# A hybrid decoder trunk on one core: four small moves in layer 0, and operand tiles placed at whole kilobytes

## The reference

```python
# layer 0: a recurrent branch beside a latent attention, one output projection
z = rms_norm(h) @ w_in                       # 1024 x 1440
xr, gate, q_lat, kv_lat, k_rope = split(z)
y_lru = rg_lru(xr, gate)                     # conv of 4 taps, two sigmoid gates, a scan over tokens
q  = rms_norm(q_lat) @ w_qb                  # 8 heads of 64 + 32 (rotary)
kv = rms_norm(kv_lat) @ w_kvb                # 64 for keys, 64 for values per head
y_mla = causal_softmax_attention(q, k, v)
h = h + concat(y_lru, y_mla) @ w_out
# layer 1: mLSTM in chunks instead; after either layer
u = causal_conv3(rms_norm(h) @ w_up)         # 1024 -> 2 x 2816
h = h + (silu(u_gate) * u_value) @ w_down
```

## Time and profile before

| | us |
|---|---|
| median of 3 runs | 2345.33 (2345.32 to 2349.07) |
| the profiled execution | 2344.9 |
| its span, first to last instruction | 2342.5 |
| TensorE busy | 2280.9 (97%) |
| VectorE busy | 1330.9 (57%) |
| GpSimd busy | 1028.1 (44%) |
| ScalarE busy | 903.5 (39%) |
| DMA | 122 MB, 52 GB/s over the span |

### The profile page before, as it was taken

How to read it: one execution, slowest core, us unless ns; L and a number is a source line. 1 busy time by engine, 2 the same in 40 slices (tenths; PEclk the granted TensorE clock), 3 DMA queues, 4 the chain that set the end, 5 groups by cost and what they waited for, 6 DMA issues and landing times.

```text
span 2342.5 us, 31827 instructions
## 1 busy us (share of the span) xinstructions
PE 2280.9 (97%) x10415; PEld 1853.4 (79%) x10415; DVE 1330.9 (57%) x2181; ACT 903.5 (39%) x1595; POOL 1028.1 (44%) x711
## 2 busy tenths in 40 slices
PE   8998999999999999999999999999999999999997
PEld 6686777778888888888878878878788888888886
DVE  6846565258655555555671115663875555555556
ACT  4535555124433333333441114451443333333333
POOL 2413333423555555555443422224335555555554
PEclk9999999999999999999999999999999999999998
DMA  5100000311111111111231110012101111111112
GB/s 180 42 18 1 1 0 28 117 36 46 39 52 54 54 49 49 48 50 54 69 124 50 45 45 28 28 73 81 30 35 55 54 54 52 46 51 47 54 54 90
DMA packets 34583, 122.07 MB, mean 52 GB/s; under 512 B 3840, under 2 KB 3968, under 8 KB 34240
## 3 DMA queue, kind: packets, MB, share of 16 engines
q1 hardware_dynamic: 31616, 106.44, 14.6%
q10 hardware_dynamic: 2880, 14.49, 1.6%
HBM read 112.52 MB, written 8.39 MB: 52 GB/s over the span
## 4 chain that ended last, share of the span: by engine, by line
PE 87%; DVE 6%; ACT 3%; issue 2%; POOL 1%; DMA 1%; SPq 0%; ACTq 0%; DVEq 0%; POOLq 0%
PE ps L816 10%; PE ps L814 10%; PE ps L818 9%; PE ps L736 9%; PE ps L738 9%; PE ps L737 9%; PE ps L854 6%; PE ps L855 6%; PE ps L856 6%; PE ps L1572 2%; PE ps L1719 1%; PE ps L1723 1%; PE ps L1721 1%; PE ps L1560 1%; DMA stage<-in_wt 1%
## 5 line engine op out<-in xcount | busy, mean ns | idle before, releaser
L516 POOL TENSOR_TENSOR wlo<-stage,whi 128x512 fp32r<-128x512 f32 x308 | 397.5, 1296 | 462.3 <-ACT whi L979 457.7
L736 PE MATMUL ps<-ahi,whi 128*128 128x512 f32 x896 | 368.5, 411 | 17.3 <-DVE alo L2239 10.3
L435 POOL TENSOR_TENSOR whi<-stage,cons 128x1024 fp32r<-128x1024 f32 x64 | 127.4, 1991 | 548.6 <-PE ps L738 338.2
L738 PE MATMUL ps<-ahi,wlo 128*128 128x512 f32 x896 | 350.4, 391 | 0.0
L737 PE MATMUL ps<-alo,whi 128*128 128x512 f32 x896 | 350.0, 391 | 0.0
L979 ACT CAST whi<-stage 128x512 fp32r<-128x512 f32 x308 | 189.1, 620 | 363.6 <-POOL stage L529 180.6
L1239 DVE TENSOR_TENSOR hT<-hT,ps 128x512 f32<-128x512 f32 x352 | 238.7, 685 | 153.9 <-PE ps L856 153.9
L854 PE MATMUL ps<-hid_hi,whi 128*128 128x512 f32 x640 | 252.2, 394 | 0.7 <-POOL wlo L516 0.2
L855 PE MATMUL ps<-hid_lo,whi 128*128 128x512 f32 x640 | 249.8, 390 | 0.0
L856 PE MATMUL ps<-hid_hi,wlo 128*128 128x512 f32 x640 | 249.7, 390 | 0.0
L814 PE MATMUL ps<-ahi,whi 128*128 128x512 f32 x608 | 236.7, 389 | 0.0
(11 more groups left out here) (324 smaller groups left out, 4096.9 us busy)
## 6 DMA issues: line engine op xcount, KB each, us to landing
stage<-in_wt SPq DMA_DIRECT2D x184, 512.0 KB, 3.6
hT<-in_xt SPq DMA_DIRECT2D x16, 256.0 KB, 6.9
hT<-in_xt ACTq DMA_DIRECT2D x8, 512.0 KB, 7.5
spill<-hT ACTq DMA_DIRECT2D x1, 4096.0 KB, 12.1
hT<-spill ACTq DMA_DIRECT2D x8, 512.0 KB, 8.6
out<-hT SPq DMA_DIRECT2D x16, 256.0 KB, 2.1
wqb_s<-in_wqb ACTq DMA_DIRECT2D x1, 1024.0 KB, 5.2
wlru_s<-in_wlru SPq DMA_DIRECT2D x1, 512.0 KB, 10.8
```

The costliest lines, as they stand in the source:

```text
L516: nc.gpsimd.tensor_tensor(block_lo(c), src, block_hi(c).bitcast(F32), ALU.subtract).then_inc(sem(L + "b_ready"), 1)
L736: nc.tensor.matmul(bank, hi, rhs_k[0][:, tok], start=k_first, stop=False)
L738: return nc.tensor.matmul(bank, lo, rhs_k[0][:, tok], start=False, stop=k_last)
```

## The change

It has five parts. First, the arena: `base` is rounded to 128 bytes, `nw` is rounded up to a whole kilobyte (109 KB), and `xc`, `rt2`, `qf`, `upg`, `upv`, `cvg` and `h1` get new offsets; all pieces, `hid_hi` and `hid_lo`, `lat` and the attention's tiles then start at whole kilobytes, `upv` does not. Second, `reduced()` goes behind `branch_conv(0)`, `branch_in(1)` and `gate_in(0)`. Third, GpSimd makes the rests of all four recurrent outputs, VectorE none. Fourth, ScalarE's list at the start of the attention has another order: `lat_hi` is made later, one tile at a time, each after GpSimd's rest of the tile whose place it takes. Fifth, the recurrent part of output tile m = 0 (eight `product3`, four feature tiles by two token halves) is issued between the steps 4 to 7 of the last head, into banks 2 and 4; the rest of that tile follows behind the head.

```diff
@@ arena
-        base = -(-nc.sbuf_base // 32) * 32
+        base = -(-nc.sbuf_base // 128) * 128
-        nw = -(-c0 // 32) * 32
+        nw = -(-c0 // KB) * KB
-        xc = at("xc", sh + 36 * KB + 32, [P, S])
+        xc = at("xc", sh + 37 * KB, [P, S])
-        upg = at("upg", f1, [P, S + 2])
-        upv = at("upv", f1 + 4 * KB + 32, [P, S + 2])
-        cvg = at("cvg", f1 + 8 * KB + 64, [P, S])
-        h1 = f1 + 12 * KB + 64
+        cvg = at("cvg", f1, [P, S])
+        h1 = f1 + 4 * KB
+        upg = at("upg", h1 + 34 * KB, [P, S + 2])
+        upv = at("upv", h1 + 38 * KB + 32, [P, S + 2])
@@ GpSimd
-            for n, j in enumerate((0, 1)):
-                lru_rest(j, n + 3)
+            for j in range(LRU_T):
+                lru_rest(j, j + 1)
@@ VectorE
             branch_in(0)
-            reduced()
             branch_conv(0)
             branch_in(1)
             gate_in(0)
+            reduced()
...
-            for n, j in enumerate((2, 3)):
-                dve.wait_ge(sem("act_hi"), n + 1)
-                nc.vector.tensor_tensor(alo[:, j, :], ylru[:, j, :], ahi[:, j, :].bitcast(F32),
-                                        ALU.subtract).then_inc(sem("dve_lat"), 1)
@@ VectorE, dve_out
-                    nc.vector.tensor_tensor(h, h, ps[:, 2 * (1 - m % 2) + s, :], ALU.add).then_inc(sem(L + "res"), 1)
+                    bank = 2 + 2 * s if m == 0 else 2 * (1 - m % 2) + s
+                    nc.vector.tensor_tensor(h, h, ps[:, bank, :], ALU.add).then_inc(sem(L + "res"), 1)
@@ ScalarE
-            for j in (2, 3, 0, 1):
+            for j in range(LRU_T):
                 nc.scalar.copy(ahi[:, j, :], ylru[:, j, :]).then_inc(sem("act_hi"), 1)
...
-            act.wait_ge(sem("dve_lat"), 4)
-            for k in range(2):
+            values_out(3)
+            act.wait_ge(sem("dve_lat"), 2)
+
+            def latent_hi(k):
+                act.wait_ge(sem("lru_split"), k + 3)
                 nc.scalar.copy(lat_hi[:, k, :], lat[:, k, :]).then_inc(sem("act_hi"), 1)
-            values_out(3)
+
+            first_query_hi(0, 1)
             nope(0, 0, first_banks[0], 3)
             values_out(4)
-            first_query_hi(0, 1)
+            latent_hi(0)
+            values_out(5)
+            latent_hi(1)
+            values_out(6)
             first_query_hi(1, 0)
-            values_out(5)
-            for c in range(6, TT):
-                values_out(c)
+            values_out(7)
@@ TensorE
+            fillers = {4: ((0, 0),), 5: ((0, 1), (1, 0)), 6: ((0, 2), (1, 1)), 7: ((0, 3), (1, 2), (1, 3))}
+
+            def out_filler(s, k):
+                if (s, k) == (0, 0):
+                    pe.wait_ge(w_ready, T_L0_OUT + 1)
+                    pe.wait_ge(sem("lru_split"), LRU_T)
+                product3(ps[:, 2 + 2 * s, :], slice(k * P, (k + 1) * P), slot_of(T_L0_OUT),
+                         (ahi[:, k, :], alo[:, k, :]), k == 0, False, halves[s])
...
+                    if last and par == 1 and k in fillers:
+                        for filler in fillers[k]:
+                            out_filler(*filler)
                     weigh(p * 2 + par, k, step, grp)
...
-            for m in range(KT):
+            for s in range(2):
+                pe.wait_ge(sem("L0res"), s + 1)
+                for k in range(LRU_T, KT):
+                    last_pair_turned(k, s)
+                    mm = product3(ps[:, 2 + 2 * s, :], slice(k * P, (k + 1) * P), slot_of(T_L0_OUT),
+                                  (ahi[:, k, :], alo[:, k, :]), False, k == KT - 1, halves[s])
+                mm.then_inc(half_done if s == 0 else w_used, 1)
+            for m in range(1, KT):
```

More of the change, by code:

```diff
@@ L183, in build @@
         rt1 = at("rt1", sh + 32 * KB, [P, S])
-        rt2 = at("rt2", sh + 36 * KB + 32, [P, S])
-        qf = [at(f"qf{s}", sh + (34 + 4 * s) * KB + 32 * s, [P, HALF]) for s in range(2)]
+        rt2 = at("rt2", sh + 36 * KB, [P, S])
+        qf = [at(f"qf{s}", sh + (34 + 4 * s) * KB, [P, HALF]) for s in range(2)]
         kf = at("kf", sh + 53 * KB, [P, S])
@@ L1505, in project @@
                     pe.wait_ge(sem("wh_rest"), h)
-                    pe.wait_ge(sem("dve_lat"), 6)
+                    pe.wait_ge(sem("dve_lat"), 4)
                 if part in (0, 3):
@@ L1614, in _ @@
                 values(c)
-            pe.wait_ge(sem("dve_lat"), 4)
+            pe.wait_ge(sem("dve_lat"), 2)
             project_first(1, first_banks[1])
@@ L1628, in _ @@
             head_pair(HEADS // 2 - 1, last=True)
-            pe.wait_ge(sem("lru_split"), 2)
             pe.wait_ge(sem("y_read"), len(turns) * (HEADS // 2 - 1) + 1)
@@ L1640, in sums_within @@
                     pe_spread(pe, "F0n", 0, diagf)
-            for m in range(KT):
+            for s in range(2):
[6 more added lines that the diff above has]
+            for m in range(1, KT):
                 m_tile(pe, T_L0_OUT + m, (T_L0_OUT + m) % RING, (2 * (1 - m % 2), 2 * (1 - m % 2) + 1),
                        lambda s: pe.wait_ge(sem("L0res"), 2 * m + s + 1),
-                       last_pair_turned if m == 0 else sums_within if m == KT - 1 else None)
+                       sums_within if m == KT - 1 else None)
             pe_mlp(pe, "F0", T_FFN0, "n1")
```

## The result

The changed kernel takes **2329.1 us** (median of 6 runs, 2326.0 to 2331.3) against 2345.5 us: a ratio of **0.9928, with a 95% interval of 0.9917 to 0.9939**. The prediction was 2326.7 us, in a range of 2319.5 to 2333.5. The profiled execution took 2326.8 us, with a span of 2324.5 us against 2342.5. It is one of the quicker ones: its 18.1 us (2344.9 - 2326.8) are 1.8 us more than the medians show, so a difference of a microsecond or two between two traces is no evidence of a part's worth.

A forecast was written before the change was run, and what follows sets the result against it. TensorE was taken to bound the kernel, busy 2280.9 of 2342.5 us. Gains of 4.8 + 2.1 + 5.1 + 6.6 = 18.6 us off 2344.9, with 0.4 for the median, gave 2326.7 us, 8-in-10 range 2319.5 to 2333.5.

The forecast's parts named there:

- Part 1: Recurrent branch: reduced() moved behind the convolution and gates ends TensorE's wait for xrp; gain 4.8 us, bounds 2.5 to 7.1.
- Part 2: Attention start: rests on GpSimd gain nothing, ScalarE's new order brings first scores earlier; gain 2.1 us, bounds 0.4 to 4.2.
- Part 3: Last head: eight products fill TensorE's waits and the clock stays full; gain 5.1 us, bounds 2.5 to 5.6.
- part of a rival: Rival "Less comes back": VectorE keeps slack at tile 7, kf isn't held, no clock falls; 2321.8 us, chance 0.15.
- Part 4: Feed-forward and latent products: tiles at whole kilobytes make matmuls faster; gain 6.6 us, bounds 4.2 to 9.
- Nothing covers this time, so all of it is gained: Feed-forward part: the 0.16 us saved per run of up_blocks, 38 runs, counts in full, 6.1 us.
- 64 bytes short of a kilobyte: Feed-forward product T3: ten or more operands lie so at nw; T2 and T3 take 0.11 us above twice B11's time.
- the address is not the cause: Rival on the layout: 64 bytes change nothing, the layout gains nothing; 2333.3 us, chance 0.12.
- The upper bound of 9 us: Layout's largest gain: 1368 matmuls at 6.6 ns, the cost in a run with all operands off the boundary.
- the fourth rival: "Slower": rate follows distance between tiles read together, new places slow products reading moved tiles; 2355 to 2363 us, chance 0.03.
- The rival that named the failure of part 4 by its effect, 2333.3: The rival "the address is not the cause": layout gains nothing, 2345.3 - 12.0 = 2333.3 us, chance 0.12.
- the signs that the prediction named: Right: xrp wait gone, lg wait at tile 7, kf after a rest, scores earlier, full clock, T2 and T3 in 5.44 us.

The follow-up runs named there:

- e3_rests: Kernel before with only GpSimd making all four recurrent rests and ScalarE's new order ahead of the attention: 2341.0 us, ratio 0.9979.
- e4_head: Kernel before with only the eight output products put into the last head: 2340.9 us, ratio 0.998.
- e8_cast: Changed kernel with ScalarE rounding the sixth weight block earlier, in the second up_blocks of each feed-forward pair: 2321.8 us, ratio 0.9904 to the kernel before.
- e5_base64: Changed kernel with everything in SBUF 64 bytes further, distances between tiles kept: 2330.2 us in one run.
- e6_steps: Changed kernel with only the pieces moved, to different offsets from their whole kilobyte: 2332.9 us in one run.

## Why the prediction was right, and where it wasn't

**Part 1, forecast 4.8 us, alone 6.6 (4.0 to 9.8), so not resolved from the forecast.** The steps held: the wait for `xrp` went, the second convolution ended at 76.1 (forecast 76.2), the second gates came 7.1 us earlier (forecast 7.1), and the new wait stood before tile 7. It is 1.5 us and not 2.3, since `gate_in(2)` ended at 105.9 and not at 106.6. What the forecast didn't have is a half clock at 164 to 166 us, which takes 1.6 to 3.3 us in the traces that have it; fewer and shorter ones later give about as much back. Neither is shown to be this part's doing.

**Part 2, forecast 2.1 us, alone 4.6 (2.8 to 7.0).** `kf` was held by a rest as forecast, and the scores came 2.9 us earlier against the norm instead of 2.1. Of the half clock from 197 to 207.5 the forecast says "I leave that as it is"; it is 3.4 us long in the changed kernel and in e3_rests, which is worth about 2 us in these traces. But e4_head lacks it with the old order, so the order isn't shown to have shortened it, and where the rest of the 4.6 us above the scores' 2.9 comes from stays open.

**Part 3, forecast 5.1 us, alone 4.6 (2.6 to 6.8).** From the weighting of step 4 on the lead grows from 10.5 to 15.6 us, which is 5.1. The weightings came 0.3, 1.2, 0.4 and 1.0 us later, 3.0 in sum, where the forecast had 3.1. The clock stayed full. Ahead of it the half clocks at the starts of three pairs of heads went as well, which I had only as part of a rival: the lead grows there from 8.4 to 10.5 us, less than the slow stretches were worth, since TensorE at full clock waits at each start for the turned pair's `alo` (1.9 us in three, in the list above). That the three are gone isn't shown to be the change's doing: e8_cast, the same program up to 500 us, has two of them.

**Part 4, forecast 6.6 us, alone 0.7 (-0.2 to 4.0), and none that can be measured on top of the others.** The rate was right: 0.17 us for each run of `up_blocks` (forecast 0.16). Two steps of the argument failed. "Nothing covers this time, so all of it is gained", with its reason that VectorE and GpSimd "have idle time in every stretch of this part and can follow", is the one that cost 6 us. GpSimd is idle for more than half of the span, but in a chain of eight steps over three engines' queues idle time means nothing; the number to look for was the slack at the point where the chain meets TensorE. It could be read from the trace of before, where the rest that the down products need ended 0.1 to 0.3 us ahead of them in all 18 pairs, and TensorE already started them up to 0.4 us late in 11. In the list of waits, where it would have had to be noticed, that is one short row (us in total, times, longest):

```profile
PE ps L854 <- POOL wlo L516: 0.2, 1, 0.2
```

Here a row of 0.2 us in a periodic place marked an engine that had just caught up, not one that had room.

The other failed step is that the slow rate belongs to tiles "64 bytes short of a kilobyte": the address alone costs nothing (e5_base64). The reading behind it was off as well. Of T3's twelve moving operands nine lie at `nw`, not "ten or more"; of T2's ten lie at whole kilobytes, not half, and still nine of its twelve intervals are off the fast rate. That spoke more strongly for the rival "the address is not the cause" than its chance of 0.12. (The upper bound of 9 us takes 6.6 ns a matmul; 2.79 against 2.72 us over twelve is 5.8, and 8 us.) The mechanism of the fourth rival, that the distance between tiles counts, is nearer to what the runs show; its sign was wrong, since the new layout puts all the tiles at whole kilobytes from each other. The Trainium skill's page "SBUF — State Buffer" (Operand start alignment) asks for no more than the element size, and says of this rule that it is about legality and not speed. Nothing here goes against the rule. On speed, a shift of everything by 64 bytes costs nothing in the traces (2.72 us per product both times), and tiles at different remainders do cost (2.79 against 2.72 us for T3).

**The sum.** 18.6 forecast and 16.3 measured: 6 us too many in part 4, and some 4 too few in parts 1 and 2. The total fell within 2.4 us of the forecast because these cancel, which is luck. The rival that named the failure of part 4 by its effect, 2333.3, was 4 us off for the opposite reason. Of the signs that the prediction named, all "right" ones were there, T2 and T3 in 5.44 us among them (of `kf` the row shows only its longer time and its end behind the third rest): a sign that a mechanism works isn't a sign that it pays.

## What to carry to other kernels

Before a faster engine is credited with its time, look at the slack of whatever it meets at the end of each period, not at the busy shares: if a chain over other queues ends within 0.3 us of it, the gain stops there. Then look for the one step of that chain that stands behind unrelated work in its queue; moving it cost nothing here, and turned a gain too small to measure into some 6.5 us. Time parts alone and in pairs (with and without the suspected cover), since a right total can hide two wrong terms. And before a half clock's coming or going is put down to a change, look for a kernel without the change that shows the same.

## What the runs showed of the hardware

- 512-column fp32r matmuls start every 226.7 ns when all operands lie at whole kilobytes from each other, also with everything 64 bytes further (e5_base64). In T2 and T4 of the kernel before, where two of twelve moving operands lie 64 bytes off the others, they start every 231 ns in the mean (226 to 236 each), and nine of the twelve intervals are off. In e6_steps nine intervals on tiles at whole kilobytes are still off behind T3.
- A half clock can come without an idle stretch ahead of it: at 165.9 us of the changed kernel TensorE's last wait, of 0.9 us, was at 106 us. Where half clocks fall differs between kernels whose program is the same up to there: up to 400 us the kernel before has 27 us of them (five places, the longest 10.2 us), e4_head 14 us (two places). A part's gain of 1 to 3 us can't be read from one trace for that reason.
- A half clock ahead of a wait costs nothing. In the kernel before TensorE ran slow from 2320.2 to 2323.6 us and then waited 2.2 us for the last norm's `diag`; in the changed kernel it ran at full clock there and waited 3.7 us. Of a lead of 20.4 us 18.8 were left behind this wait.
